# Pairs of tiles: VectorE adds a norm's tiles, TensorE sums only what is left over the partitions

## What is computed

```python
def rms_norm(x, g):
    y = x * rsqrt(mean(x * x, axis=-1) + EPS) * g
def layer_norm(x, g, b):                       # conformer_conv's, and layer_norm_2 alike
    mu = mean(x, axis=-1); xc = x - mu
    y = xc * rsqrt(mean(xc * xc, axis=-1) + EPS) * g + b
# first block
u = rms_norm(h, mix_pre_g);  proj = u @ w_in
... attention, and: z = layer_norm(conv(a * sigmoid(b)), ln_g, ln_b); y_conv = silu(z) @ w_conv_o
h = h + rms_norm(merged @ w_out, mix_post_g)                 # "p1"
h = h + rms_norm((silu(gate) * up) @ w_down, ffn_post_g)     # "p2"
# second block, two layers
x = layer_norm_2(ALPHA * x + even_layer(x), ...)             # ends in @ ev_w_out, "l1"
x = layer_norm_2(ALPHA * x + odd_layer(x), ...)              # ends in @ w_o, "l2"
```

## Time and profile before

| | |
|---|---|
| median of 3 timed runs | 2597.49 us (2597.24 to 2598.43) |
| profiled execution, its own time | 2594.56 us |
| its span | 2592.8 us |
| TensorE matmuls busy | 2500.0 us, 96% |
| VectorE busy | 1566.5 us, 60% |
| ScalarE busy | 1170.8 us, 45% |
| mean granted TensorE clock | 0.987 of full speed |

### The profile page before, as it was taken

One profiled execution on the slowest core, in us unless ns is written; L12 is line 12 of the kernel. 1 busy time (PEld: TensorE's weight loads), 2 busy tenths in 40 slices (PEclk: granted clock), 3 DMA queues, 4 the chain that ended last, 5 costly groups with the idle time before them and its releaser, 6 DMA issues.

```text
span 2592.8 us, 38168 instructions
## 1 busy us (share of the span) xinstructions
PE 2500.0 (96%) x15470; PEld 2149.8 (83%) x15470; DVE 1566.5 (60%) x2116; ACT 1170.8 (45%) x1547; POOL 72.1 (3%) x94
## 2 busy tenths in 40 slices
PE   8999999999899999999999899989899999999896
PEld 7888888888788888888887788878787888888685
DVE  6888887764665665655444657555622674356555
ACT  5444554644444444444433455563536201255544
POOL 0000000000000000000000000000000201011000
PEclk9999999999999999999999999999999999999998
DMA  6665556555355566655555455535533456322362
GB/s 231 189 188 155 166 168 195 163 186 172 96 189 184 186 191 195 193 188 188 183 187 175 143 170 178 178 121 185 196 114 111 142 168 206 130 91 83 110 216 89
DMA packets 419456, 427.69 MB, mean 165 GB/s; under 512 B 25345, under 2 KB 414465, under 8 KB 418321
## 3 DMA queue, kind: packets, MB, share of 16 engines
q1 hardware_dynamic: 414880, 403.07, 48.9%
q0 software_dynamic: 4400, 22.19, 2.6%
HBM read 415.19 MB, written 9.96 MB: 164 GB/s over the span
## 4 chain that ended last, share of the span: by engine, by line
PE 79%; DVE 12%; ACT 5%; issue 2%; DMA 2%; SPq 0%; ACTq 0%; DVEq 0%
PE GP L1791 72%; PE SB L1791 7%; DVE wL L1011 4%; ACT wH L495 2%; DVE y L1011 1%; DVE acc L1017 1%; DMA raw<-w_gate_up_dram 1%; DMA raw<-w_in_dram 1%; DVE x L1011 1%; DVE j L1011 1%; DVE f L1017 1%; DVE ga L1011 0%; PE SB L1795 0%; DMA raw<-w_o_dram 0%; SPq L474 0%
## 5 line engine op out<-in xcount | busy, mean ns | idle before, releaser
L1011 DVE TENSOR_TENSOR wL<-raw,wH 128x1024 fp32r<-128x1024 f32 x664 | 804.0, 1226 | 581.1 <-ACT wH L495 580.0
L495 ACT CAST wH<-raw 128x1024 fp32r<-128x1024 f32 x664 | 683.7, 1047 | 566.3 <-PE GP L1791 305.4
L1791 PE MATMUL GP<-u2B,wH 128*128 128x512 f32 x1408 | 443.5, 396 | 0.0
L1791 PE MATMUL GP<-uB,wH 128*128 128x512 f32 x1152 | 362.9, 396 | 0.0
L1791 PEld LDWEIGHTS GP<-u2B,wL 128*128 128x128 f32 x1408 | 264.7, 189 | 71.8 <-issue 4.6
L1791 PE MATMUL GP<-u2B,wL 128*128 128x256 f32 x1408 | 279.3, 280 | 5.9 <-DVE u2B L1017 5.2
L1791 PEld LDWEIGHTS GP<-uB,wL 128*128 128x128 f32 x1152 | 216.1, 189 | 55.2 <-DVE wL L1011 3.9
L1791 PE MATMUL GP<-xB,wH 128*128 128x512 f32 x768 | 243.4, 398 | 0.0
L1791 PE MATMUL GP<-uB,wL 128*128 128x256 f32 x1152 | 232.2, 283 | 4.6 <-DVE wL L1011 3.2
L1791 PE MATMUL GP<-xk,dw 128*128 128x256 f32 x1024 | 230.6, 383 | 5.7 <-DVE xk L1017 5.7
L1791 PEld LDWEIGHTS GP<-xk,dw 128*128 128x128 f32 x1024 | 195.7, 192 | 34.8 <-issue 7.5
(11 more groups left out here) (399 smaller groups left out, 3086.8 us busy)
## 6 DMA issues: line engine op xcount, KB each, us to landing
raw<-w_gate_up_dram SPq DMA_DIRECT2D x352, 256.0 KB, 3.7
raw<-w_in_dram SPq DMA_DIRECT2D x288, 256.0 KB, 3.5
raw<-ev_w_in_dram SPq DMA_DIRECT2D x192, 256.0 KB, 3.4
raw<-w_down_dram SPq DMA_DIRECT2D x176, 256.0 KB, 3.4
raw<-w_out_dram SPq DMA_DIRECT2D x64, 256.0 KB, 3.6
raw<-ev_w_out_dram SPq DMA_DIRECT2D x64, 256.0 KB, 3.3
dw<-w_k_dram SPq DMA_DIRECT2D x64, 256.0 KB, 3.3
dw<-w_r_dram SPq DMA_DIRECT2D x64, 256.0 KB, 3.2
```

Of the source, the lines that this page charges most:

```text
L495: e.copy(wH[SLOT[i]], raw[m % RAW].rearrange("p (k n) -> p k n", k=4)).then_inc(s["hi"], 1)
L1011: return e.tensor_tensor(o, a, b, op)
L1791: return e.matmul(o, l, r, start=start, stop=stop, skip_group_check=True)
```

## The change

VectorE adds tiles elementwise until two of them are left, and TensorE sums only these two over the partitions.

- p1 and p2: ScalarE writes the squares of slab 0 into a new tile `sum1` or `sum3`; one unit after each of slabs 1 to 6 ends, VectorE adds that slab's squares to it. TensorE sums this pair at the place of slab 6, and the squares of slab 7 behind it.
- `conv_norm`: VectorE adds the 8 tiles of `acc` in halves (4 + 4, 2 + 2) into `csq` in a 121st step of the task `conv`, late in w_in. After the Square it adds the 8 tiles of `csq` in the same way, in its step 3, at unit 2. TensorE waits for these adds.
- l1 and l2: VectorE adds each slab's `y` to `ysum` behind slabs 1 to 5; TensorE sums this pair once. In `centre`, step 5, VectorE adds the squares 4 + 4, + 4, then 2 + 2; TensorE sums two tiles in step 6. Its steps 3 to 5 are empty.

New semaphores `sq_sum` and `y_sum` count the adds. The diff, cut to its core:

```diff
-("conv", i + 15, 120, 1)
+("conv", i + 15, 121, 1)
...
+SUMMED = {"p1": 0, "p2": 6, "l1": 0, "l2": 8}
...
@@ ScalarE, empty_post @@
-                    if j > 1:
-                        e.wait_ge(s[key + "_st"], j - 1)
-                    e.activation(sqb[:, 2 * (j % 2):2 * (j % 2) + 2, :], o, ACT.Square).then_inc(s[key + "_sq"], 1)
+                    if j > 2:
+                        e.wait_ge(s["sq_sum"], SUMMED[key] + j - 2)
+                    to = sqb[:, 2 * (j % 2):2 * (j % 2) + 2, :] if j else total
+                    e.activation(to, o, ACT.Square).then_inc(s[key + "_sq"], 1)
...
@@ VectorE, stream @@
+                    if behind and u - 1 in ENDS and ENDS[u - 1] >= N0[name]:
+                        behind(ENDS[u - 1] - N0[name])
                     side(u)
...
@@ VectorE, end of conv @@
+                e.wait_ge(s["cv"], 248)
+                tt(csq[:, 0:4, :], acc[:, 0:4, :], acc[:, 4:8, :], ALU.add).then_inc(s["cv"], 1)
+                e.wait_ge(s["cv"], 249)
+                tt(csq[:, 0:2, :], csq[:, 0:2, :], csq[:, 2:4, :], ALU.add).then_inc(s["cv"], 1)
+                yield
...
@@ VectorE, conv_norm, step 3 @@
+                e.wait_ge(s["cn_act"], 2)
+                tt(csq[:, 0:4, :], csq[:, 0:4, :], csq[:, 4:8, :], ALU.add).then_inc(s["cv"], 1)
+                e.wait_ge(s["cv"], 251)
+                tt(csq[:, 0:2, :], csq[:, 0:2, :], csq[:, 2:4, :], ALU.add).then_inc(s["cv"], 1)
...
@@ VectorE, p1 and p2 @@
+            def squares(sqb, total, key):
+                def behind(j):
+                    if 0 < j < 7:
+                        e.wait_ge(s[key + "_sq"], j + 1)
+                        if j > 1:
+                            e.wait_ge(s["sq_sum"], SUMMED[key] + j - 1)
+                        tt(total, total, sqb[:, 2 * (j % 2):2 * (j % 2) + 2, :], ALU.add).then_inc(s["sq_sum"], 1)
+                return behind
...
@@ VectorE, empty_ln, j < 6 @@
+                        if j:
+                            e.wait_ge(s[key + "_s"], j + 1)
+                            if j > 1:
+                                e.wait_ge(s["y_sum"], SUMMED[key] + j - 1)
+                            tt(total, total if j > 1 else y[:, 0:2, :], y[:, q, :], ALU.add).then_inc(s["y_sum"], 1)
...
@@ VectorE, centre, step 5 @@
+                for q in (1, 2):
+                    e.wait_ge(s[key + "_sq"], q + 1)
+                    if q > 1:
+                        e.wait_ge(s["y_sum"], SUMMED[key] + 6)
+                    tt(sqb[:, 0:4, :], sqb[:, 0:4, :], sqb[:, 4 * q:4 * q + 4, :], ALU.add).then_inc(s["y_sum"], 1)
+                e.wait_ge(s["y_sum"], SUMMED[key] + 7)
+                tt(sqb[:, 0:2, :], sqb[:, 0:2, :], sqb[:, 2:4, :], ALU.add).then_inc(s["y_sum"], 1)
+                yield
...
@@ TensorE, conv_norm @@
-                e.wait_ge(s["cv"], 248)
+                e.wait_ge(s["cv"], 250)
                 e.wait_ge(s["at_dve"], 64)
-                stat(SB[0][:, 0:256], [acc[:, j, :] for j in range(8)], True, True).then_inc(s["cn_pe"], 1)
+                stat(SB[0][:, 0:256], [csq[:, j, :] for j in range(2)], True, True).then_inc(s["cn_pe"], 1)
...
-                e.wait_ge(s["cn_act"], 2)
-                stat(SB[1][:, 0:256], [csq[:, j, :] for j in range(8)], True, True).then_inc(s["cn_pe"], 1)
+                e.wait_ge(s["cv"], 252)
+                stat(SB[1][:, 0:256], [csq[:, j, :] for j in range(2)], True, True).then_inc(s["cn_pe"], 1)
...
@@ TensorE, post_stat @@
-                    e.wait_ge(s[key + "_sq"], j + 1)
-                    stat(SB[0][:, 0:256], [sqb[:, 2 * (j % 2) + i, :] for i in range(2)], j == 0, j == 7).then_inc(s[key + "_st"], 1)
+                    if j == 6:
+                        e.wait_ge(s["sq_sum"], SUMMED[key] + 6)
+                        stat(SB[0][:, 0:256], [total[:, i, :] for i in range(2)], True, False).then_inc(s[key + "_st"], 1)
+                    if j == 7:
+                        e.wait_ge(s[key + "_sq"], 8)
+                        stat(SB[0][:, 0:256], [sqb[:, 2 + i, :] for i in range(2)], False, True).then_inc(s[key + "_st"], 1)
...
@@ TensorE, ln_sum @@
-                    if j < 6:
-                        e.wait_ge(s[key + "_s"], j + 1)
-                        stat(SB[0][:, 0:256], [y[:, 2 * j + i, :] for i in range(2)], j == 0, j == 5).then_inc(s[key + "_st"], 1)
+                    if j == 5:
+                        e.wait_ge(s["y_sum"], SUMMED[key] + 5)
+                        stat(SB[0][:, 0:256], [total[:, i, :] for i in range(2)], True, True).then_inc(s[key + "_st"], 1)
...
@@ TensorE, centre @@
-                yield
-                yield
-                for q in range(3):
-                    e.wait_ge(s[key + "_sq"], q + 1)
-                    stat(SB[1][:, 0:256], [sqb[:, 4 * q + i, :] for i in range(4)], q == 0, False).then_inc(s[key + "_q"], 1)
-                    yield
+                for _ in range(5):
+                    yield
+                e.wait_ge(s["y_sum"], SUMMED[key] + 8)
+                stat(SB[1][:, 0:256], [sqb[:, i, :] for i in range(2)], True, False).then_inc(s[key + "_q"], 1)
```

More of the change, by code:

```diff
@@ L220, in _plan @@
     i, e, k = U0["w_in"], U0["ev_w_in"], U0["w_k"]
-    rows = [("scale1", i, 6, 1), ("bias", i + 3, 1, 1), ("bias", i + 8, 1, 1), ("conv", i + 15, 120, 1),
+    rows = [("scale1", i, 6, 1), ("bias", i + 3, 1, 1), ("bias", i + 8, 1, 1), ("conv", i + 15, 121, 1),
             ("attention0", i + 57, 27, 1), ("attention1", i + 84, 27, 1), ("conv_norm", U0["w_attn_o"], 8, 1),
@@ L248 @@
 kk_a kk_pe kk_mx kk_n kk dec_d dec_a dec_g sv_pe sv_dve sv_act sv_sol nd ns td back kb0 kb1 vb gb0 gb1 gb2 xb
-zero jp0 jp1 jp2 ja0 ja1 ja2 jd0 jd1 jd2 jg0 jg1 jg2 go oy_h oy_l kp l2_st l2_m l2_y l2_s l2_sq l2_q l2_t l2_u x2 out""".split()
+zero sq_sum y_sum jp0 jp1 jp2 ja0 ja1 ja2 jd0 jd1 jd2 jg0 jg1 jg2 go oy_h oy_l kp l2_st l2_m l2_y l2_s l2_sq l2_q l2_t l2_u x2 out""".split()
 def build_block(nc, d, out):
@@ L336, in build_block @@
         sq1 = blk("sq1", 4, 0, [P, 4, NT])
+        sum1 = blk("sum1", 4, 4096, [P, 2, NT])
         def gq(i):
@@ L349, in build_block @@
         sq3 = blk("sq3", 2, 0, [P, 4, NT])
+        sum3 = blk("sum3", 2, 4096, [P, 2, NT])
         xB, xH, xL = both("xB", 3, DT)
@@ L369, in build_block @@
         sq4 = blk("sq4", 6, 0, [P, DT, NT])
+        ysum1 = blk("ysum1", 3, 0, [P, 2, NT])
         o = VEC["w_dw"][0]
@@ L401, in build_block @@
         sq5 = blk("sq5", 8, 0, [P, DT, NT])
+        ysum2 = blk("ysum2", 7, 0, [P, 2, NT])
         def scratch(name, shape):
@@ L983, in scalar_program @@
             stream("w_conv_o", empty_conv)
-            stream("w_out", empty_post(f1, sq1, "p1"))
+            stream("w_out", empty_post(f1, sq1, sum1, "p1"))
             post_rt("p1")
@@ L987, in scalar_program @@
             stream("w_gate_up", empty_gu, lambda u: [u2_tile(i) for i in tile_range(u, 1)])
-            stream("w_down", empty_post(f2, sq3, "p2"))
+            stream("w_down", empty_post(f2, sq3, sum3, "p2"))
             post_rt("p2")
@@ L1031, in side, with stream @@
                         next(tasks[task], None)
-            def stream(name, empty, tiles=None, turn=None):
+            def stream(name, empty, tiles=None, turn=None, behind=None):
                 for u in range(U0[name], U1[name]):
@@ L1337, in pool_mix, with empty_ln @@
                     yield
-            def empty_ln(key, y, outx, part):
+            def empty_ln(key, y, outx, part, total):
                 def empty(n, sl, j):
@@ L1354, in empty_ln, with centre @@
                 return empty
-            def centre(key, y, outx):
+            def centre(key, y, outx, sqb):
                 e.wait_ge(s[key + "_m"], 1)
@@ L1369, in norm_head @@
                 tt(rsA, rsU, rsU, ALU.mult).then_inc(s[key + "_t"], 1)
-                e.wait_ge(s[key + "_q"], 5)
+                e.wait_ge(s[key + "_q"], 3)
                 e.wait_ge(s[key + "_t"], 1)
@@ L1597, in vector_program @@
                      "sticks1": sticks(1), "pool_windows": pool_windows(), "pool_mix": pool_mix(),
-                     "centre1": centre("l1", y1, x), "centre2": centre("l2", y2, x2),
+                     "centre1": centre("l1", y1, x, sq4), "centre2": centre("l2", y2, x2, sq5),
                      "mix1": mix(1, 0, xr), "mix2": mix(2, 3, xk), "mix3": mix(3, 5, xr),
@@ L1607, in vector_program @@
             stream("w_conv_o", empty_conv)
-            stream("w_out", empty_post(f1))
+            stream("w_out", empty_post(f1), behind=squares(sq1, sum1, "p1"))
             post_rs("p1")
@@ L1611, in vector_program @@
             stream("w_gate_up", empty_gu, lambda u: [u2_tile(i) for i in tile_range(u, 1)])
-            stream("w_down", empty_post(f2))
+            stream("w_down", empty_post(f2), behind=squares(sq3, sum3, "p2"))
             post_rs("p2")
@@ L1633, in vector_program @@
             stream("w_g", empty_g, turn=turn)
-            stream("w_o", empty_ln("l2", y2, x2, stage))
```

(9 more changed lines are left out.)

14 lines of the change are left out of this document (7 added, 7 removed).

## The result

The changed kernel took 2579.48 us (median of 4 runs, 2576.87 to 2582.62) where the kernel before took 2597.36 (4 runs, 2591.61 to 2598.43). The ratio is 0.9943, with a 95% interval of 0.9929 to 0.9956: 14.8 us less, between 11 and 18. Forecast were 23.0 us less. The sign was right, a third of the gain is missing. (The ratio weighs all the runs and is not the quotient of the two medians.

What follows compares the result with a forecast made beforehand. TensorE was taken to bound the kernel, with 79% of the chain. 32.8 us of removed matmuls, less 1.6 and 2 x 2.6 of idles, less 2 x 1.5 of clock, gave 23.0 us saved: 2574.5 us, range 2568 to 2582.

Steps and rivals of the forecast that it cites:

- The price of a ones-matmul: All tile sums on TensorE: each ones-matmul holds 0.43 us; 76 fewer give 32.8 us.
- The Trainium skill's isolated gap: Formula N/2.4 + 2.5 ns, 109 ns per matmul, 8.3 us in all, time 2589; given no chance of its own.
- p1 and p2: In w_out and w_down: 5.2 us saved each, the add for slab 6 in time with 0.8 us slack.
- The rival with more stalls: p1 and p2 lose their slack for slab 6, the conv's idle pays clock too: 8.4 us less saved, 2583; chance 0.12.
- The conv's norm: Second sum of the conv's norm: a new TensorE idle of 1.6 us, so 3.6 of 5.2 us remain.
- Centre: Both LayerNorms: TensorE idles 3.3 us for the added squares, keeping 1.7 of 4.3 us each before clock loss.
- the clock behind them: Behind each centre idle: TensorE mostly loses the full clock, 1.5 us each taken from a range of 0 to 1.8.
- What leaves TensorE's queue leaves the time: Whole kernel: TensorE holds 79% of the chain, so most of what is removed from its queue shortens the time.
- The rival of freed time that turns into waits for weights: Removed matmuls bring nothing, as freed time becomes waits for weights at the same places: 2597; chance 0.03.
- The last line of what would show the steps wrong: Forecast falls if VectorE's adds take much over 0.69 and 1.23 us, or TensorE's waits for weight splits grow.

Runs made afterwards that it cites:

- the lighter kernels: w_gate_up's 44 scalings cut to 16 of 256 columns, in the kernel before, with p1 alone changed, and in the changed kernel: 2592.27, 2585.84 and 2569.42 us.
- the kernels with one norm: Against the kernel before, only w_out's norm (p1) changed: ratio 1.0000; only the conv's norm changed: ratio 1.0006.
- the order changed in centre: Changed kernel with the sum of the added squares moved from unit 30 to behind the last unit in both LayerNorms: 2568.85 us, ratio 0.9897.

## Why the prediction was right and wrong

- **The price of a ones-matmul, 0.43 us**, was right: 0.86 for the sum that stays, and 22.9 us in all, idles and clock deducted, where w_gate_up gives nothing back. The Trainium skill's isolated gap (TensorE: Matmul & The Clock Gate, section Back-to-back issue gap) would have made the 76 matmuls an estimated 8 us; the runs refuse it.
- **p1 and p2** were right: no wait for slab 6, slack 0.77 us for 0.8; the stages fell by 5.8 and 5.2 us for 5.2 each. The rival with more stalls there did not come.
- **The conv's norm** was right: idle 1.26 us for 1.6, 3.7 us kept for 3.6, and the granted clock behind it was 1.00.
- **Centre**: the idles were right (3.77 and 3.42 us for 3.3). The term mis-sized is the clock behind them. I took 1.5 us from a range that ended at 1.8, the loss of eight units behind another idle. Here the twelve records of sums behind the idle are six matmuls, 2.6 us at 0.43, and took 5.3 in the first LayerNorm: 2.7 lost. In another profile of the changed kernel the second idle, 3.42 us again, cost none: the record behind it took 1.13 us. The second one of the first profile lost 1.8 (4.37 us on the chain). So each is 0 to 2.7 us, about the 1.5 I took; the first stretch kept 3.6 us for 4.5, the second 4.8.
- **"What leaves TensorE's queue leaves the time"** is the step that failed, in the first paragraph, and with it every term ahead of w_gate_up. I read the chain's 79% on TensorE as proof for the whole kernel, and asked of each place whether its own sum was hidden. The sum has no term for the stages between the edited ones; it puts them at nothing without a reason. 5.9 us were lost in w_gate_up and 1.7 in w_conv_o (the latter in some profiles only), of the 9.5 that both norms ahead had saved. The rival of freed time that turns into waits for weights was named, but "at the same places", judged by w_out's lead of over 4 us (4.9 to 6.7 us in the second half of that stage, but 1.4 to 3.0 at its fourth unit) and given 0.03. It held in part, one stage further on, where the lead was under 1 us in most groups of units. The last line of what would show the steps wrong, TensorE's waits for weight splits, was the one that grew, from 2.0, 5.8 and 6.3 us in the stage to 12.1, 11.2 and 15.7.

By the stages that is the whole: 23.0 - 5.9 - 1.7 and the rest within the scatter of single stages gives 15.6 us between the means of three spans (2593.5 and 2577.8), and the timed runs say 14.8. The range's upper end, 2582, allowed idles and clock, but no term for a stage behind. The changed kernel's own median, 2579.5, lies inside that range and the ratio's value, 0.9943 x 2597.4 = 2582.6, just above it; either way the range came close by its reserve for idles and clock, most of which was not needed, and not by its mechanism.

**What stays open.** That the time is lost by TensorE's waits for VectorE in w_gate_up is shown by the lighter kernels, and that changes ahead of the stage bring them by the kernels with one norm. Why a stage that is entered with the same leads, down to 0.2 us at its 16th unit, runs with less lead in the 160 units that follow is not settled; what a changed norm ahead sets off in it stays open. The place of the packets on q8 doesn't explain it, and that of the packets on q14 was not tried. The waits of ScalarE for the raw weights by DMA are longer where the stage is (147.7, 146.9 and 150.5 us in the window of the three profiles of after, against 138.2, 135.9 and 143.5), but in a loop in which the DMA waits for VectorE's split, as VectorE waits for the cast, that can be effect as well as cause.

## What to carry to other kernels

A stage counts as bound by an engine only if its feeders have lead, and the lead is read per stage: distance from the feeder's end to the reader's start. Time that is saved ahead of a stage whose lead is near zero need not come out; here nothing measurable came out for one norm alone. Before an edit, read the lead in the stages behind it too, not only in the edited one, and give the forecast a term for those without one; and where a new link must be read at the end of a stage, let the engine read first what is ready and last what is late, which here gave about 11 us for two moved lines.

## What the runs showed of the hardware

- An idle of TensorE of one and the same length, 3.42 us, was followed by sums at half the clock in one profile of the changed kernel (2.08 us for the record, granted clock 0.50) and at the full clock in another (1.13 us, granted clock 1.00). The Trainium skill (same page, section Why this matters for your kernels) warns of such idle gaps; the trace agrees in some executions only, so its price is a range that begins at 0.
- A stage that nothing in the code touches (w_gate_up) differed by 3 us between three profiles of one kernel, on at least two chips, while the stages with lead (w_down, the conv's norm) repeated within 1 us.
- 156 further wait instructions on a semaphore already at its value, in TensorE's queue, cost some 7 us ahead of w_gate_up in the kernel before, 102 only 1 to 2 in the changed one (w_out 101.0 us for 98.7, and 101.0 for 99.7 with the order changed in centre).
